# Compression keys and values of paged samples: dense page rows gathered by GpSimd, two sets of them during the projection, and a first product on half-height tiles in four jobs

## What is computed

```python
def _chunk_feats(rows, pe, w1):            # rows: (B, L, G=2, E=64), CMP_STRIDE = 16
    c = rows.reshape(B, L // CMP_STRIDE, CMP_STRIDE, G, HEAD_DIM)
    pe2 = pe.reshape(2, CMP_STRIDE, 1, HEAD_DIM)
    w = w1.reshape(2, CMP_STRIDE, HEAD_DIM, CMP_HID)      # CMP_HID = 128
    head = jnp.einsum('bnrge,ref->bngf', c + pe2[0], w[0])
    tail = jnp.einsum('bnrge,ref->bngf', c + pe2[1], w[1])
    return head, tail
def _compress_from_feats(head, tail, w2):
    return jnp.einsum('bngf,fe->bnge', jax.nn.gelu(head[:, :-1] + tail[:, 1:]), w2)
...
    past_cmp = cache_cmp[page_table].reshape(DB, PAST_LEN, 2, G_A, HEAD_DIM)
```

## Time and profile before

| what | us |
|---|---|
| median of 3 runs (lowest, highest) | 2145.36 (2137.95, 2154.14) |
| profiled execution, its own time | 2156.45 |
| its span, first to last instruction | 2154.6 |
| TensorE busy | 1894.2 (88%) |
| VectorE, ScalarE, GpSimd busy | 1111.1, 821.7, 272.2 |
| mean granted TensorE clock | 0.958 |

### The profile page before, as it was taken

One profiled execution on the slowest core, in us unless ns is written; L12 is line 12 of the kernel. 1 busy time (PEld: TensorE's weight loads), 2 busy tenths in 40 slices (PEclk: granted clock), 3 DMA queues, 4 the chain that ended last, 5 costly groups with the idle time before them and its releaser, 6 DMA issues. The chain is left out here.

```text
span 2154.6 us, 29729 instructions
## 1 busy us (share of the span) xinstructions
PE 1894.2 (88%) x10915; PEld 1555.6 (72%) x10915; DVE 1111.1 (52%) x2627; ACT 821.7 (38%) x1742; POOL 272.2 (13%) x342
## 2 busy tenths in 40 slices
PE   3998996457799868888884999999999999999997
PEld 3787775456688757777673778788778878878885
DVE  4776861122678757776774433443344344344344
ACT  4444431100678756665664323222123122222211
POOL 0000000101344434443431000000000000000000
PEclk9999997688899999999997999999999999999998
DMA  5322213661465523222224311220231121133102
GB/s 176 110 76 101 81 51 58 85 118 40 130 168 157 151 71 107 82 84 82 84 94 127 123 59 59 98 71 28 97 98 59 40 98 59 40 98 127 32 18 87
DMA packets 172326, 189.93 MB, mean 88 GB/s; under 512 B 55942, under 2 KB 139110, under 8 KB 171000
## 3 DMA queue, kind: packets, MB, share of 16 engines
q1 hardware_dynamic: 170114, 187.13, 29.9%
q10 hardware_dynamic: 2080, 1.05, 0.2%
HBM read 166.60 MB, written 59.81 MB: 105 GB/s over the span
## 5 line engine op out<-in xcount | busy, mean ns | idle before, releaser
L2419 DVE SCALAR_TENSOR_TENSOR m_conv<-m_ext,m_taps,m_conv 128x512 f32<-128x512 f32 x44 | 33.1, 751 | 371.7 <-ACT m_ext L2311 371.7
L1737 DVE CUSTOM_DVE_ANT_0 l_e<-l_s,k_masks 128x1024 f32<-128x1024 f32 (+3 forms) x192 | 138.4, 721 | 85.1 <-PE l_s L1382 75.3
L2161 PE MATMUL o_py<-f_h_hi,m_gu_hi 128*128 128x512 f32 x704 | 179.8, 397 | 0.0
L2161 PE MATMUL o_py<-f_h_lo,m_gu_hi 128*128 128x512 f32 x704 | 178.4, 395 | 0.0
L2161 PE MATMUL o_py<-f_h_hi,m_gu_lo 128*128 128x512 f32 x704 | 178.4, 395 | 0.0
L1679 ACT ACTIVATE l_e<-l_e,l_nmin 128x640 f32<-128x640 f32 (+11 forms) x224 | 169.9, 758 | 20.5 <-DVE l_nmin L1737 18.9
L1636 ACT ACTIVATE l_pT_hi<-l_t 128x512 fp32r<-128x512 f32 (+3 forms) x288 | 125.7, 472 | 120.7 <-PE l_t L1422 119.4
L2309 ACT ACTIVATE m_conv<-o_py,m_taps 128x512 f32<-128x512 f32 (+1 forms) x66 | 42.8, 648 | 333.2 <-PE o_py L2161 333.2
L1807 DVE TENSOR_TENSOR l_pT_lo<-l_t,l_pT_hi 128x512 fp32r<-128x512 f32 (+3 forms) x288 | 143.4, 526 | 27.1 <-ACT l_pT_hi L1636 26.6
L2161 PEld LDWEIGHTS o_py<-f_h_lo,m_gu_hi 128*128 128x128 f32 x704 | 131.9, 187 | 32.3
L2161 PEld LDWEIGHTS o_py<-f_h_hi,m_gu_lo 128*128 128x128 f32 x704 | 131.9, 187 | 32.3
(11 more groups left out here) (283 smaller groups left out, 3941.2 us busy)
## 6 DMA issues: line engine op xcount, KB each, us to landing
m_raw_gu<-in_w_gate SPq DMA_DIRECT2D x22, 512.0 KB, 5.4
m_raw_gu<-in_w_up SPq DMA_DIRECT2D x22, 512.0 KB, 7.1
m_raw_d<-in_w_down SPq DMA_DIRECT2D x11, 1024.0 KB, 5.0
p_raw<-in_w_in SPq DMA_DIRECT2D x5, 2048.0 KB, 8.0
c_rows<-in_cache_cmp SPq DMA_DIRECT2D x64, 128.0 KB
a_kd_k<-in_state_dil SPq DMA_DIRECT2D x8, 1024.0 KB, 8.3
a_kd_v<-in_state_dil SPq DMA_DIRECT2D x8, 1024.0 KB, 7.8
a_kd_k<-in_cache_slc SPq DMA_DIRECT2D x128, 64.0 KB, 1.8
```

Source lines behind the costliest of these rows:

```text
L1737: return nc.vector.tensor_tensor_reduce(out=dst, in0=src, in1=m, scale=1.0, scalar=CLAMP, op0=ALU.add, op1=ALU.min, accum_out=low)
L2161: last = nc.tensor.matmul(bank[q % 3][:, 0:w], ws[k][:, m, c, :], hs[:, c, t0:t0 + w], start=(j == 0 and c == 0), stop=(j == 2 and c == KC ...
```

## The change

Four jobs of two samples; job 1 has the prompt as a third part. The rows lie dense: partition p of a sample holds positions 8p' to 8p'+7 (8 KB), 16 partitions a page, and one indirect DMA of GpSimd for each sample gathers them by an index that VectorE works out at the start. The gathers of jobs 0 and 1 are issued in the projection's last group, into memory that its input tiles have left; those of jobs 2 and 3 in `prepare`. GpSimd's copies and `rows16` go. A transpose now turns one position of both heads (head 0 in rows 0 to 63, head 1 in rows 64 to 127), and the first product has 64 multiplications of 64 rows for each head and job, head 0 in the upper half of the array and head 1 in the lower, each half into its own PSUM bank, with 126 columns (189 in job 1). w1 is loaded twice, for both halves of the partitions, and `const.loads` moves to GpSimd's queue. The encodings are multiplied the other way round (`encode`). TensorE turns two jobs ahead, with three banks in place of four, and `project_kv(m)` follows `hid(m + 1)`. The page table's load and the prompt's store move.

```diff
@@ project
-                if G == 0:
-
-                    for dst, src in const.loads:
-                        sp.dma_start(dst, src).then_inc(later_in, 16)
@@ project, gpsimd
+            nc.gpsimd.dma_start(pages.lane[:], t["lane"]).then_inc(pages.table_in, 16)
+            nc.gpsimd.dma_start(pages.table[:], t["page_rows"]).then_inc(pages.table_in, 16)
+            pool.wait_ge(w_lo_done, KC)
+            for dst, src in const.loads:
+                nc.gpsimd.dma_start(dst, src).then_inc(later_in, 16)
+            pool.wait_ge(pages.index_done, 1)
+            pool.wait_ge(w_lo_done, KC + 4 * (NG - 1))
+            pages.gather(nc, t, 0)
+            pages.gather(nc, t, 1)
@@ project, vector
+            dve.wait_ge(pages.table_in, 32)
+            nc.vector.tensor_scalar(pages.index[:], pages.table[:], float(LANES), pages.lane[:, 0:1], ALU.mult, ALU.add).then_inc(pages.index_done, 1)
@@ compress_constants
-    k.w1 = sb("k_w1", [P, 2, 16, P])
+    k.w1 = sb("k_w1", [P, 2, CMP_LEN, P])
+        for g in range(GA):
+            k.loads.append((k.w1[g * E:(g + 1) * E, c], t["w1_cmp_" + x].rearrange("(r e) f -> e r f", e=E)))
@@ Pages (new)
+    def gather(self, nc, t, m):
+        src = t["cache_cmp"].rearrange("b (l p) c g e -> (b l) (p c g e)", l=LANES)
+        for i in range(2):
+            n = 2 * m + i
+            nc.gpsimd.indirect_dma_start(self.rows(m, i), None, src,
+                                         bass.IndirectOffsetOnAxis(self.index[:, n:n + 1], 0)).then_inc(self.rows_in[m % 2], 16)
@@ prepare, sync
-            load_rows(0)
+            sp.dma_start(rows_p[:].rearrange("p a c n -> p (a c n)"),
+                         o["cmp_prompt"].rearrange("b s c g e -> (b s) (c g e)").rearrange("(p a) n -> p (a n)", p=P)).then_inc(rows_p_in, 16)
-            ld.q(0)
-            ld.kv(0)
-            ld.kd(0, 0)
-            for m in range(2, JOBS):
-                sp.wait_ge(rows_ready, 4 * (m - 1))
-                load_rows(m)
-                if m == 2:
-                    ld.q(1)
-                    ld.kv(1)
-                    ld.kd(0, 1)
+            for n in range(2):
+                ld.q(n)
+                ld.kv(n)
+                ld.kd(0, n)
@@ prepare, gpsimd
-                    nc.gpsimd.tensor_copy(rows16[0:r, k, :].rearrange("p (r e) -> p r e", e=E), rows[m % 2][0:r, :, k, :]).then_inc(rows_ready, 1)
+            for m in range(2, JOBS):
+                pool.wait_ge(t_filled, chunk(m - 1, 0))
+                pages.gather(nc, t, m)
@@ prepare, tensor
             def hid(m):
...
                 for c in range(2):
-                    for j in range(16):
-                        at = j // 8
...
-                        last = nc.tensor.matmul(hidden[m % 2][:, c, 0:n, 0:NCMP], w1[:, c, j, :], src, start=(j == 0), stop=(j == 15))
+                    for r in range(CMP_LEN):
+                        for g in range(GA):
+                            hp = slice(g * E, (g + 1) * E)
+                            x = xT[m % 2][hp, c, 0:parts(m), r % CMP_STRIDE, r // CMP_STRIDE:r // CMP_STRIDE + NCMP]
+                            last = nc.tensor.matmul(hid_at(m, c, g), w1[hp, c, r, :], x, start=(r == 0), stop=(r == CMP_LEN - 1))
...
+            def encode():
+                for c in range(2):
+                    for r in range(CMP_LEN):
+                        hp = slice(r % 2 * E, (r % 2 + 1) * E)
+                        last = nc.tensor.matmul(hidden[0][r % 2][0:1, c * 256:c * 256 + P], peT[hp, c, r:r + 1], w1[hp, c, r, :],
+                                                start=(r < 2), stop=(r >= CMP_LEN - 2))
+            encode()
+            turn(0)
...
+            turn(1)
             for m in range(JOBS):
                 hid(m)
-                if m + 1 < JOBS:
-                    turn(m + 1)
-                if m == 0:
+                if m == 1:
                     pe.wait_ge(pe_copied, 1)
-                project_kv(m)
+                if m >= 1:
+                    project_kv(m - 1)
+                if m + 2 < JOBS:
+                    turn(m + 2)
+            project_kv(JOBS - 1)
```

More of the change, by code:

```diff
@@ L630, in prepare @@
         sem = lambda name: ctx.enter_context(nc.semaphore(name))
-        q_new = sb("c_q_new", [NS, 2, 512])
+        q_new = sb("c_q_new", [P, 2, 512])
         k_new = sb("c_k_new", [NS, 512 + 2 * P])
[L633 to L638, removed]
@@ L651, in prepare, with parts, chunks_of @@
         block = ctx.enter_context(nc.Block())
[L653 to L657, removed]
+        def parts(m):
+            return 3 if m == PROMPT else 2
+        def chunks_of(m):
+            return [(c, i, quad) for c in range(2) for i in range(parts(m)) for quad in range(2)]
+        new = len(chunks_of(0))
+        chunk = lambda m, n: n if m == 0 else 4 + sum(len(chunks_of(x)) for x in range(m)) + n
         @block.sync
@@ L775, in _, with encode_turn @@
+            def encode_turn():
+                pe.wait_ge(bias_copied, 1)
+                for c in range(2):
+                    for x in range(2):
+                        last = nc.tensor.matmul(small[:, c:c + 1], bias_rows[0:1, c, x, :], ident[0:1, 0:1], start=(x == 0), stop=(x == 1))
+                last.then_inc(bias_done, 1)
+            encode()
+            turn(0)
             pe.wait_ge(new_in, 48)
             for n in range(2):
-                dst = slot(n)
+                dst = slot(new + n)
@@ L778, in _ @@
                 for j in range(4):
[L779 removed]
+                    last = nc.tensor.transpose(dst[:, j * NS:(j + 1) * NS], q_new[0:NS, n, j * P:(j + 1) * P], ident[0:NS, 0:NS])
                 last.then_inc(t_filled, 1)
[L781 to L783 removed]
@@ L784, in _ @@
-            last.then_inc(pe_done, 1)
             pe.wait_ge(kn_in, 48)
             for n, (a0, a1) in enumerate(((0, 4), (4, 6))):
-                dst = slot(2 + n)
+                dst = slot(new + 2 + n)
                 for j in range(a0, a1):
@@ L833, in _ @@
             copy = lambda dst, src: nc.vector.tensor_copy(dst, src)
-            dve.wait_ge(zeroed, 3)
-            dve.wait_ge(t_filled, 1)
+            dve.wait_ge(pe_done, 1)
+            for x in range(2):
+                ins = copy(bias_rows[0:1, :, x, :], hidden[0][x][0:1, :].rearrange("p (c n) -> p c n", c=2)[:, :, 0:P])
+            ins.then_inc(bias_copied, 1)
+            for n in range(0, len(chunks_of(0)), 2):
+                take(dve, copy, 0, n)
+            dve.wait_ge(zeroed, 2)
+            dve.wait_ge(t_filled, new + 1)
+            bank = new % TURNS
             for g in range(2):
@@ L852, in _ @@
-            dve.wait_ge(pe_copied, 1)
+                    ins = copy(b.bd_nsa[hp, :, (g * RA + r) * DT:(g * RA + r + 1) * DT], turned[bank][hp, r * NS:(r + 1) * NS].rearrange("p (b t) -> p b t", t=DT))
+            ins.then_inc(t_evac[bank], 1)
+            dve.wait_ge(bias_done, 1)
+            copy(pe_bias[:], small[:, 0:2]).then_inc(pe_copied, 1)
+            ch.step(nc.vector.tensor_scalar(w2[:], w2[:], 0.5, None, ALU.mult))
+            for n in range(0, len(chunks_of(1)), 2):
+                take(dve, copy, 1, n)
@@ L863, in _ @@
                 nc.vector.tensor_tensor(y, y, x, ALU.mult).then_inc(tanh_in, 1)
-                if m + 1 < JOBS:
-                    for n in range(0, 8, 2):
-                        take(dve, copy, m + 1, n)
+                if m + 2 < JOBS:
+                    for n in range(0, len(chunks_of(m + 2)), 2):
+                        take(dve, copy, m + 2, n)
                 dve.wait_ge(tanh_done, m + 1)
```

269 lines of the change are left out of this document (142 added, 127 removed).

## The result

| what | before | after |
|---|---|---|
| median of the comparison (lowest, highest), 4 runs each | 2143.03 (2137.95, 2154.14) | 2087.34 (2082.72, 2092.64) |
| profiled execution, its span | 2156.45, 2154.6 | 2092.64, 2090.8 |
| preparation begins, attention begins | 349.6, 546.2 | 366.5, 477.5 |
| preparation; from attention's begin to the end of the span | 196.7; 1608.4 | 111.0; 1613.3 |
| mean granted clock | 0.958 | 0.963 |

What follows compares the result with a forecast made beforehand. The preparation was taken as bound by page-row transfers, afterwards by TensorE; walking TensorE's order moved attention's begin from 546.2 to 463.3, so 2145.36 - 83 = 2062 us, with a range of 2048 to 2116.

Steps and rivals of the forecast that it cites:

- the walk: Preparation, ten steps along TensorE's order: attention begins at 463.3 in place of 546.2, 83 us gained; chance 0.62.
- `turn(2)`: Preparation, step 6: VectorE's bias and gelu's first half 3.0, banks 3.5, wait for job 2's gather 2 us.
- `project_kv(0)` and `turn(3)`: Preparation, step 8: 1 us, then 4.0 + 3.5 behind VectorE's copies and wider gelu.
- The end: Preparation, step 10: last `project_kv(2)`, bias, kv copies, gelu, tanh, second product and copy, 8 us.
- The price of a pair: First product: two half-height records side by side cost the larger of load 111 and product 108 ns; 163 in job 1.
- the two rules that were weighed: First product: load time goes by columns alone (serial loads), or different tiles load and multiply in parallel (the walk).
- What else moves: Outside the preparation: constants on GpSimd's queue 0; gathers beside the last group's stores 0 to 3 us, 0 taken.
- the serial loads: First product, rival: weight loads go one after the other, 28.4 us a job, gain 33, time 2112; chance 0.16.
- the slow gathers: Preparation, rival: gathers take 45 us or more for 2 MB, job 2 waits 23, time 2100 to 2115; chance 0.05.
- the signs that it named for itself: Profile: 256 records in some 14 us, half loads within some 10 ns, preparation some 115 us, projection ending at 346.
- nothing overlapping: First product and `encode`, rival: job 1 costs 41.7 us, 13 gained, time 2132; chance 0.08.
- GpSimd too slow: Constants' loads, rival: some 9000 pieces ahead of the gathers; at 50 ns each, time 2225; chance 0.06.

Runs made afterwards that it cites:

- experiment 3: The changed kernel with head 0's 32 first-product multiplications issued all before head 1's, for keys and for values: 2145.99 us, ratio 0.9952.
- after again: The changed kernel, unedited, run again beside two other kernels on one chip: 2084.76 us, ratio 0.9671.
- experiment 5: The changed kernel with its four projection gathers apart and w1 cut into sixteen 256 KB loads, one per finished tile from the third: 2071.70 us, ratio 0.9604.
- experiments 2: The changed kernel with its four last-group gathers issued one at a time, the later ones after two, four and six tiles: 2082.51 us, ratio 0.9646.
- experiment 8: The changed kernel with gathers apart and w1 loaded for the first head alone, the other half set to zero: 2080.50 us, ratio 0.9648.
- experiments 2 and 7: The second of these: the changed kernel with jobs 0 and 1's gathers issued at the preparation's start, not in the projection: 2084.82 us, ratio 0.9665.
- the later sets: Three sets of follow-up runs, each beside the kernel before the change, whose medians were 2156.62, 2156.6 and 2161.24 us.
- experiment 1: The changed kernel with the constants (masks, w1 twice, w2, encodings) issued by SyncE again, not GpSimd: 2095.57 us, ratio 0.9696.

## Why the prediction was right in its kind and 25 us off in its size

**Step by step through the walk** (forecast; measured in the timeline of after): `encode` 9; 8.8. `turn(0)` 4.5; 4.0. New tokens 3.6; 3.3. `turn(1)` 6.0; 5.8. `hid(0)` 14.2; 14.5. `turn(2)` 8.5 with a gather wait of 2; 6.4 with none. `hid(1)` 20.9; 20.7. `project_kv(0)` and `turn(3)` 8.5; 9.4, the clock being at half for its last 4 us. `hid(2)` to `hid(3)` 30.1; 30.3. The end 8; 7.9. Sum 113.3 (the prediction's end time has 113.7); 111.0. The stage was right because the steps that make up most of it were counts of records times a row. The small steps were estimates: the gather wait of 2 us wasn't there, and `turn(3)`, with a wait of 2.7 us for VectorE and the half clock behind it, took 0.9 more than forecast.

**The price of a pair.** Forecast 111 ns from column tiles. In after's trace the loads of the two halves begin at 395.093 and 395.100, and the next pair at 395.205: 112 ns for a pair. On the two rules that were weighed: the Trainium skill's page TensorEngine Tiling (Array Packing), section Key Properties (different tiles load and multiply in parallel), held for row tiles too, as long as their instructions alternate (experiment 3); the page TensorE: Matmul & The Clock Gate of the same skill, section LDWEIGHTS, which has a load's time go by columns, holds within one tile (a load of 64 rows by 128 columns took 188 ns, where 128 by 128 had 192), and read as one path for all it would have given 28 us a job. What sets the pair, its 126 columns (108) or its load (111), isn't told apart at that size; at 189 columns it is the product, 162 ns a pair.

**The failed step: "What else moves".** Two terms of the sum were taken at 0, with a bound of +5, and measured 17 together (13 in after again).
- "TensorE didn't wait for these; no gain, no loss", of the constants. It is a loss of 7 to 10: the last group begins at 305.7 in after and at 297.2 with sixteen loads (experiment 5). The doubled bytes alone don't explain it, as half of them still cost 4.9 of the 7.4 us between the starts of experiments 2 and 5 (experiment 8).
- "0 to 3 us, 0 taken, since a slot is wanted again 10 us later", of the gathers. The 10 us run from the copy into the slot. The store is issued 7.5 us after that copy in the first group, and what is left to it before the next tile is summed is 3.2 us, there and in the last group. Four gathers between two copies cost 7 to 8 (experiments 2 and 7), or 4 where the clock doesn't fall.

The rows to see it were there: a finished tile's copy, its store's issue, and the copy two tiles later stand in the timeline of the projection of before:
```profile
58.76 0.60 ACT L307 ACTIVATE p_z<-p_pz 128x512 f32<-128x512 f32 x1 [9.02 <-PE p_pz L359]
...
66.16 17.50 SPq L248 DMA_DIRECT2D scratch_qa<-p_z  x4
69.64 0.60 ACT L307 ACTIVATE p_z<-p_pz 128x512 f32<-128x512 f32 x1 [1.59 <-PE p_pz L359]
```
They give 3.5 us from a store's issue to the copy that needs its slot. The prediction read none of them, and priced the transfers by how busy the DMA engines were on average (0.14 busy).

**The rest of the 25.** 2145.36 - 85.7 + 16.9 is 2076.6; the comparison gave 2087.3, 10.8 more. Of these 4.9 are the longer rest behind the preparation. The other 5.8 come from the base: before's profiled execution was 11.1 above the median that the forecast started from, and after's only 5.3 above its own. Both lie in the spread of the executions, and before's is the wider: its median in the comparison was 2143.0, and 2156.6, 2156.6 and 2161.2 in the later sets, while after had 2087.3 and 2084.8. With the last set's before, the gain is 76.5.

**What was luck.** The walk's own bounds were 2050 to 2080, and 2087 lies outside them. It lies in the range up to 2116 only because the range was drawn over the serial loads and the slow gathers, and neither happened. No case of the prediction gives 2087. Of the signs that it named for itself, the pairs' cost, the 7 ns between their loads, the stage's length and the missing waits for rows came true; the projection's end at 346 didn't (363).

**The rivals.** Loads one after the other and nothing overlapping: false as the kernel is built, and experiment 3 shows the second's price, 27.8 us a job (28.4 forecast for the serial loads) and a gain of 11 us (13 forecast; the interval allows 1 to 20). GpSimd too slow: false by far; it issued two loads of 1 MB in 512-byte pieces and a small one in 2.80 us, under 1 ns a piece, against a bound of 28, and the last of them had landed by about 84 us. The port that VectorE shares, which the page SBUF — State Buffer of the Trainium skill names under SBUF: two separate sides, showed no stretched issue here; the loads themselves were slow, but no faster from SyncE's queue (experiment 1). Slow gathers in the stage: false; nobody waited for the rows of jobs 2 and 3. What did go wrong in the projection was in none of the rivals, though its place was named among the terms.

## What to carry to other kernels

When a transfer is put beside a pipeline that stores its results, look up one store: when it is issued, when its buffer is wanted, and what is queued by then. That slack, and not the mean share of the DMA engines, says how much may be queued at once. Cutting a load and letting it go by the pipeline's own count left at most 1.6 us of the loss here. Two tiles of half height pay only while their instructions alternate, so a change to them is to be judged in the order of the loops first.

## What the runs showed of the hardware

- Two row tiles of 64 ran fp32 products together: 256 records of 126 columns in 14.56 us in turn, 27.82 us one tile after the other (experiment 3).
- 3.56 MB in 512-byte pieces filled 97% of the DMA engines' time over 20 us, at 197 GB/s in all; a 256-KB store issued into this on another queue landed 11 us later.
- GpSimd issued 1 MB of such pieces in about 1 us; SyncE needed 29 us for the four of them. An indirect gather of 1 MB (128 rows of 8 KB) took about 1 us to issue; of four in flight the last two landed 11.2 and 12.4 us after theirs.
- TensorE's next products after a wait could run at the lower clock: 3.78 us for eight records after 5.68 us without work, and again after 4.46, where 1.98 is usual, so these waits cost more than their length. After 3.60 us in the repeat they ran at the full one, 2.11 us.
